# S5's reciprocal and stores placed anew, its scan laid out with group pairs innermost, biases and S5's copies on ScalarE, the last rows stored by halves

## What is computed

```
for layer in 0, 1:
    x = norm0(a * x + 0.5 * swiglu_1(x))
    x = norm1(a * x + mix(x))          # layer 0: MoBA attention || retention;  layer 1: S5 + GLU
    x = norm2(a * x + 0.5 * swiglu_2(x))
S5: lam_bar = exp(lam * dt);  b_bar = (lam_bar - 1) / lam * b
    s[t] = lam_bar * s[t-1] + b_bar u[t]   (64 groups x 64 complex states)
    y[t] = real(c s[t]) + d * u[t]
```

## Time and profile before

| | us |
|---|---|
| median of 3 runs | 2661.59 |
| the profiled execution: time | 2662.27 |
| its span (first to last instruction) | 2660.6 |
| PE busy | 2451.7 (92%) |
| DVE busy | 1674.6 (63%) |
| ACT busy | 1013.3 (38%) |
| POOL busy | 605.6 (23%) |
| mean granted TensorE clock | 0.965 |

### The profile page before, as it was taken

One profiled execution on the slowest core, in us unless ns is written; L12 is line 12 of the kernel. 1 busy time (PEld: TensorE's weight loads), 2 busy tenths in 40 slices (PEclk: granted clock), 3 DMA queues, 4 the chain that ended last, 5 costly groups with the idle time before them and its releaser, 6 DMA issues.

```text
span 2660.6 us, 45493 instructions
## 1 busy us (share of the span) xinstructions
PE 2451.7 (92%) x18333; PEld 2301.8 (87%) x18333; DVE 1674.6 (63%) x2676; ACT 1013.3 (38%) x1496; POOL 605.6 (23%) x658
## 2 busy tenths in 40 slices
PE   6998498999899889999999999999999979989995
PEld 6998497999788767779889999999999978989995
DVE  4786375657765544567676658567556685576554
ACT  2443134433354333344253433454333425343332
POOL 5487630000420012210121401023102220242003
PEclk9999799999999999999899999999999989999997
DMA  8657366543453678645446555555554646544452
GB/s 174 182 160 194 91 190 189 150 120 114 124 146 112 207 225 261 170 121 145 111 143 187 168 153 175 179 158 143 155 150 143 194 136 197 157 143 135 143 149 77
DMA packets 675394, 417.25 MB, mean 157 GB/s; under 512 B 31250, under 2 KB 639378, under 8 KB 675186
## 3 DMA queue, kind: packets, MB, share of 16 engines
q1 hardware_dynamic: 668658, 393.98, 51.6%
q0 software_dynamic: 6528, 20.37, 2.5%
HBM read 395.51 MB, written 18.78 MB: 156 GB/s over the span
## 4 chain that ended last, share of the span: by engine, by line
PE 70%; DVE 14%; POOL 5%; issue 4%; ACT 4%; DMA 3%; SPq 2%; POOLq 0%; ACTq 0%; DVEq 0%
PE ps L255 18%; PE ps L256 18%; PE ps L257 18%; DVE w_lo L250 3%; ACT w_hi L241 2%; PE ps L838 2%; PE ps L840 2%; PE ps L839 2%; POOL arena L1964 2%; PE ps L2192 1%; PE ps L1533 1%; POOL x L551 1%; PE ps L1548 1%; DVE arena L2292 1%; PE ps L1575 1%
## 5 line engine op out<-in xcount | busy, mean ns | idle before, releaser
L250 DVE TENSOR_TENSOR w_lo<-w_raw,w_hi 128x1024 fp32r<-128x1024 f32 (+1 forms) x648 | 821.3, 1273 | 658.7 <-ACT w_hi L241 655.1
L255 PE MATMUL ps<-x_hi,w_hi 128*128 128x256 f32 (+1 forms) x3200 | 973.3, 304 | 60.7 <-DVE w_lo L250 51.7
L256 PE MATMUL ps<-x_lo,w_hi 128*128 128x256 f32 (+1 forms) x3200 | 959.0, 300 | 0.0
L257 PE MATMUL ps<-x_hi,w_lo 128*128 128x256 f32 (+1 forms) x3200 | 958.2, 299 | 0.0
L241 ACT ACTIVATE w_hi<-w_raw 128x1024 fp32r<-128x1024 f32 (+1 forms) x648 | 668.3, 1034 | 561.3 <-PE ps L257 398.6
L255 PEld LDWEIGHTS ps<-x_hi,w_hi 128*128 128x128 f32 x3200 | 619.8, 194 | 78.2 <-DVE w_lo L250 64.8
L256 PEld LDWEIGHTS ps<-x_lo,w_hi 128*128 128x128 f32 x3200 | 619.9, 194 | 1.4 <-issue 0.2
L257 PEld LDWEIGHTS ps<-x_hi,w_lo 128*128 128x128 f32 x3200 | 619.1, 193 | 0.0
L255 PE MATMUL ps<-h_hi,w_hi 128*128 128x256 f32 (+1 forms) x1408 | 425.9, 303 | 15.7 <-DVE w_lo L250 11.1
L256 PE MATMUL ps<-h_lo,w_hi 128*128 128x256 f32 (+1 forms) x1408 | 416.0, 295 | 0.0
L257 PE MATMUL ps<-h_hi,w_lo 128*128 128x256 f32 (+1 forms) x1408 | 416.0, 295 | 0.0
(11 more groups left out here) (257 smaller groups left out, 2361.5 us busy)
## 6 DMA issues: line engine op xcount, KB each, us to landing
w_raw<-in_ffn_w_gate SPq DMA_DIRECT2D x176, 512.0 KB, 4.3
w_raw<-in_ffn_w_up SPq DMA_DIRECT2D x176, 512.0 KB, 3.9
w_raw<-in_ffn_w_down SPq DMA_DIRECT2D x128, 512.0 KB, 4.0
w_raw<-in_w_in_ab SPq DMA_DIRECT2D x56, 512.0 KB, 3.9
w_raw<-in_ffn_w_down SPq DMA_DIRECT2D x64, 384.0 KB, 3.4
arena<-in_cache_v POOLq DMA_DIRECT2D x64, 256.0 KB, 4.5
arena<-in_cache_k SPq DMA_DIRECT2D x64, 256.0 KB, 3.8
w_raw<-in_w_out_ab SPq DMA_DIRECT2D x16, 512.0 KB, 3.8
```

The source lines that it names most:

```text
L250: dve.tensor_tensor(T.w_lo[:, u % RING, 0:n], T.w_raw[:, u % RAW, 0:n], T.w_hi[:, u % RING, 0:n].bitcast(F32), ALU.subtract).then_inc(T.w_ ...
L255: pe.matmul(out, w_hi, m_hi, start=first, stop=False)
L256: pe.matmul(out, w_hi, m_lo, start=False, stop=False)
L257: return pe.matmul(out, w_lo, m_hi, start=False, stop=last)
```

## The change

1. `size2`'s reciprocal is made on DVE inside `S5Constants.vector` (four more small instructions there, three fewer on POOL), and the copies of the reversed powers go from step 10 to step 7 with a semaphore of their own, `fallen`. POOL makes `b_bar` first and waits for `fallen` afterwards. PE turns c at step 5 instead of 10.
2. `prepare.load` issues b in 16 DMAs of 32 KB, two a weave step, then c, in weave steps 0 to 8, where SP had only the weights. Decays are stored at lag -3 instead of 5, taps at lag 4.
3. `start` is laid out `[128, re/im, chunk, pair]`. `advance` has 6 instructions; the first product and the first sum take both parts at once. The carry is added run by run: DVE takes runs 0 and 1 (1 alone for A, whose first carry is zero), POOL runs 2 and 3.
4. ACT, instead of DVE, copies `u` from PSUM and makes both halves of `stack`.
5. ACT, instead of POOL, adds the bias in all twelve norms: at norm steps 5 and 6 behind DVE's scaling where no products follow, at steps 7 and 8 behind DVE's L511 otherwise (POOL did it at 8 and 9).
6. The very last norm (`alone`) sums its squares by 8 accumulating products with the ones matrix on PE, into another PSUM bank; POOL has no part in it.
7. The output goes by column halves: PE turns the first 4 feature tiles as soon as those have their bias, DVE and ACT copy by turns, SP stores 6 pieces for B.

```diff
@@ Norm
+            if i == 4 and self.alone:
+                for k in range(KT):
+                    pe.wait_ge(T.squared.h, self.squared + k + 1)
+                    pe.matmul(self.root_of, T.ones[:, :], T.sq[:, k % 4, 0:self.g.n], start=(k == 0), stop=(k == KT - 1))\
+                      .then_inc(T.sq_added.h, 1)
...
+            if i in (5, 6):
                 for k in range(4 * i - 20, 4 * i - 16):
                     act.wait_ge(T.normed.h, self.normed + k + 1)
...
+                        act.activation(self.x(k), self.x(k), ACT.Identity, bias=self.bias(k)).then_inc(T.affine_done.h, 1)
+            if i in (7, 8) and self.products:
+                for k in range(4 * i - 28, 4 * i - 24):
+                    act.wait_ge(T.x_ready.h, self.ready + k + 1)
+                    act.activation(self.x(k), self.x(k), ACT.Identity, bias=self.bias(k)).then_inc(T.affine_done.h, 1)
...
-                    pool.tensor_scalar(self.x(k), self.x(k), self.bias(k), None, ALU.add).then_inc(T.affine_done.h, 1)
@@ store
+    for i, (t, q, m) in enumerate(halves(g)):
         n = after + i
+        pe.wait_ge(T.affine_done.h, whole - 4 + 4 * q)
...
+        sp.wait_ge(T.y_moved[n % 2].h, n // 2 + 1)
+        dst = y_prompt[t * P:(t + 1) * P, :] if t < PT else y_sample
+        sp.dma_start(dst[:, q * 512:(q + 1) * 512], rows[0:m, t, q * 512:(q + 1) * 512]).then_inc(T.stored.h, 16)
@@ S5Prepare
-    TURN_C = 10
+    FALL, TURN_C = 7, 5
...
+        for n in range(KT):
+            a = slice(A4 * n, A4 * (n + 1))
+            for r, part in enumerate(("re", "im")):
+                q.dma_start(self.b_raw[:, r, a], self.I["s5_b_" + part][0].rearrange("(a s) p h -> (s p) a h", s=2)[:, a])\
+                 .then_inc(self.S.b_loaded.h, 16)
+            yield
...
-            q = self.at(i, 5)
+            q = self.at(i, -3)
             if q is not None:
                 sp.wait_ge(S.c_done.h, q + 1)
...
+            q = self.at(i, 4)
+            if q is not None:
                 sp.wait_ge(S.placed.h, q + 1)
...
-                pool.wait_ge(S.inverted.h, 1)
                 tt(S.coef[:, :, :], S.coef[:, :, :], S.size2[:, :].unsqueeze(1).to_broadcast([P, 2, GPAIRS]), ALU.mult)
...
+                pool.wait_ge(S.fallen.h, 1)
                 pool.wait_ge(S.c_placed.h, 1)
@@ S5Group
+        eng.tensor_tensor(both, src, f[0].unsqueeze(1).to_broadcast([P, 2, *shape]), ALU.mult)
+        eng.tensor_tensor(buf[0], src[:, 1], f[1], ALU.mult)
+        chain(eng, eng.tensor_tensor(buf[1], src[:, 0], f[1], ALU.mult))
+        chain(eng, eng.tensor_tensor(out, out, both, ALU.add))
+        eng.tensor_tensor(out[:, 0], out[:, 0], buf[0], ALU.subtract)
+        chain(eng, eng.tensor_tensor(out[:, 1], out[:, 1], buf[1], ALU.add))
...
+        for b in (0, 1):
+            if b or self.before is not None:
+                self.fix(dve, T.dve_chain, self.part, b)
             yield
...
+                for s in range(2):
+                    self.stack(act, copy, e + 1, s)
```

More of the change, by code:

```diff
@@ L450, with __init__ @@
     STEPS = 10
-    def __init__(self, T, g, row, scale, products):
+    def __init__(self, T, g, row, scale, products, alone=False):
+        self.alone = alone
         self.T, self.g, self.row, self.products = T, g, row, products
@@ L460, in __init__ @@
         self.sq_added, self.var, self.rooted, self.normed = (
-            c.take(k) for c, k in ((T.sq_added, KT - 1), (T.var_done, 1), (T.rstd_ready, 2), (T.normed, KT)))
+            c.take(k) for c, k in ((T.sq_added, KT if alone else KT - 1), (T.var_done, 1), (T.rstd_ready, 2), (T.normed, KT)))
         self.affine, self.rounded, self.ready = (
@@ L537, in gpsimd @@
         for i in range(self.STEPS):
-            if i in (1, 2):
+            if i in (1, 2) and not self.alone:
                 for k in range(max(4 * i - 4, 1), 4 * i):
@@ L2222, in stack @@
         for r in range(2):
-            last = copy(to[HALF[r], s], self.start[HALF[s], r, pairs, :])
+            last = copy(to[HALF[r], s], self.start[HALF[s], r, :, pairs].rearrange("p c a -> p a c"))
         last.then_inc(S.stacked[s].h, 1)
@@ L2272, in scalar @@
             if e is not None and e + 1 < KT:
-                self.stack(act, copy, e + 1, 0)
+                for s in range(2):
+                    self.stack(act, copy, e + 1, s)
             if self.before is not None:
@@ L2282, in scalar, with advance @@
             yield
-    def over(self, r, k, shape):
-        f = self.jump[:, r, k]
-        return f.unsqueeze(2).to_broadcast(shape) if len(shape) == 3 else f
-    def advance(self, eng, chain, buf, out, src, f):
-        for i, (r, w) in enumerate(((0, 0), (1, 0), (1, 1), (0, 1))):
-            last = eng.tensor_tensor(buf[i], src[r], f[w], ALU.mult)
-        chain(eng, last)
-        eng.tensor_tensor(out[0], out[0], buf[0], ALU.add)
-        chain(eng, eng.tensor_tensor(out[1], out[1], buf[1], ALU.add))
-        eng.tensor_tensor(out[0], out[0], buf[2], ALU.subtract)
-        chain(eng, eng.tensor_tensor(out[1], out[1], buf[3], ALU.add))
-    def bufs(self, place, shape):
+    def advance(self, eng, chain, place, out, src, f, shape):
         n = int(np.prod(shape))
@@ L2302, in bufs, with over, fix @@
         sizes = {f"d{i}": k for i, k in enumerate(shape)}
[L2303 to L2318 removed]
+        both = place[:, 0:2 * n].rearrange(f"p (r {names}) -> p r {names}", r=2, **sizes)
+        buf = [place[:, i * n:(i + 1) * n].rearrange(f"p ({names}) -> p {names}", **sizes) for i in (2, 3)]
+        eng.tensor_tensor(both, src, f[0].unsqueeze(1).to_broadcast([P, 2, *shape]), ALU.mult)
[4 more added lines that the diff above has]
+        chain(eng, eng.tensor_tensor(out[:, 1], out[:, 1], buf[1], ALU.add))
+    def over(self, k, shape):
+        f = [self.jump[:, r, k] for r in range(2)]
+        return [x.unsqueeze(1).to_broadcast([P, *shape]) for x in f] if len(shape) == 2 else f
+    def runs(self):
+        return self.start[:, :, 0:CHUNKS_P, :].rearrange("p r (b j) a -> p r b j a", j=RUN)
+    def fix(self, eng, chain, place, b):
+        runs, shape = self.runs(), [RUN - 1, GPAIRS]
+        self.advance(eng, chain, place, runs[:, :, b, 1:], runs[:, :, b, 0:1].to_broadcast([P, 2, *shape]),
+                     [self.jump[:, r, 0:RUN - 1] for r in range(2)], shape)
     def vector(self, dve):
@@ L2342, in vector @@
                                   ALU.subtract).then_inc(S.rested.h, 1)
-            e = self.out_at(i, 1)
-            if e is not None and e + 1 < KT:
-                self.stack(dve, dve.tensor_copy, e + 1, 1)
             yield
@@ L2379, in scan @@
         yield
-        for a0 in (0, self.FIX):
-            self.fix(dve, T.dve_chain, self.part, a0)
+        for b in (0, 1):
+            if b or self.before is not None:
+                self.fix(dve, T.dve_chain, self.part, b)
             yield
         if self.before is not None:
-            advance([self.ends[:, r].rearrange("p b a -> p a b") for r in range(2)],
-                    [self.start[:, r, :, CHUNKS_P:] for r in range(2)], 0, [P, GPAIRS, DEC_BATCH])
+            advance(self.ends, self.start[:, :, CHUNKS_P:, :], 0, DEC_BATCH, GPAIRS)
             dve.memset(self.part[:, 1023:1024], 0.0).then_inc(S.ends_done.h, 1)
@@ L2741, in _ @@
             load_tables(T, M, sp, I)
-            prepare.load(sp)
-            weave(ffn(ffn_sync, sp, f0a + f0b[:1]), after(idle(1 + KT), prepare.sync(sp)))
+            weave(ffn(ffn_sync, sp, f0a + f0b[:1]), after(prepare.load(sp), prepare.sync(sp)))
             run(project_sync(T, sp, PA))
@@ L2813, in _ @@
             weave(ffn(ffn_scalar, act, f3a[2:]), N4B.scalar(act))
-            weave(ffn(ffn_scalar, act, f3b), N5A.scalar(act))
-            run(N5B.scalar(act))
+            weave(ffn(ffn_scalar, act, f3b), after(N5A.scalar(act), store_scalar(T, act, A, y_rows, before[A])))
+            run(after(N5B.scalar(act), store_scalar(T, act, B, y_rows, before[B])))
         @block.vector
```

151 lines of the change are left out of this document (66 added, 85 removed).

## The result

The changed kernel takes **2605.24 us** (2602.03 to 2605.82) against 2663.13 for the kernel before beside it: a ratio of 0.978, 95% interval 0.976 to 0.979, or 57.9 us less. The forecast was 2583 us: faster, but with 79 us to gain. The profiled execution has a span of 2603.2 us (2660.6 before) and a mean granted clock of 0.975 (0.965 before). PE is busy 2446.0 us (2451.7 before), DVE 1638.9, ACT 1085.3 and POOL 470.4.

What follows compares the result with a forecast made beforehand. PE was taken as the bound, busy 2451.7 of 2660.6 us, with DVE the bound in B's scan. Terms 47 + 15.5 + 4.7 + 7 + 8 - 3 = 79 off 2662.3, less 0.7, gave 2583 us; range 2564 to 2612.

Steps and rivals of the forecast that it cites:

- The first stage: Beside the first feed-forward, up to the projection: loads, early powers, stores, clock and projection together save 47 us (35 to 54).
- Reversed powers early: -11.7: First feed-forward: POOL's earlier powers shrink PE's 21.6 us wait for residual sums to about 10, saving 11.7 us.
- the loads in pieces: Early first feed-forward: b's 16 pieces end a 6.9 us weight wait, 4.5 us plus 1.5 for half clock: -6.
- the step of the stores: First feed-forward: decays stored eight steps earlier, apart from the taps, no longer hold up weights on SP: -6.4 us.
- unhindered, octets 0 to 3: POOL's reversed powers in the first feed-forward: without hindrance, octets 0 to 3 done at 196 us, 21.4 us each.
- R1: Rival, 14%: POOL or SP keep the first stage slow, 24 us an octet; only 20 of 47 us come: 2610.
- B's scan: Shorter VectorE scan instructions and fixes, with ScalarE's share of stack and a little clock, save 15.5 us (9 to 20).
- The sign named for PE's idle time: In B's scan, PE's idle time was to fall from 20.0 to about 5 us.
- A's scan: Nearly covered by PE's longer steps; waits of 3.66 and 1.8 us show, so -4.7 us (2 to 5).
- what is late next: First feed-forward, once PE's wait for the sums shrinks to about 10 us: POOL's own work is late next.
- charged 3 us for everything: Biases on ACT delay its next rounding, for which DVE and PE wait: a cost of 3 us (0 to 10).
- R2: Rival, 12%: layout is nothing, strides cost nothing; B saves 5 us, A 2, so 13 less: 2596.

Runs made afterwards that it cites:

- run 2: Kernel before plus only b's loads in 16 pieces and the decays' and taps' stores placed anew: 2626.9 us, ratio 0.9861.
- run 3: Kernel before plus the early reciprocal and reversed powers, the loads in pieces and the stores placed anew, nothing else: 2620.9 us, ratio 0.9834.
- run 4: Kernel before plus only the new scan: layout of start, six instructions an advance, fix by runs; u and stack copies as before: 2652.0 us, ratio 0.9956.
- run 6: Changed kernel with the biases of all layer norms back on GpSimd: 2607.24 us, ratio 0.9789.
- run 1: Kernel before plus only the early reciprocal, with the copies of the reversed powers and the turn of c five steps earlier: 2664.79 us, ratio 1.0004.
- run 8: Changed kernel with start back in its old layout (chunks innermost), six instructions an advance and fix by runs kept: 2620.54 us, ratio 0.9833.
- run 5: Changed kernel with two of the four stack copies of an octet back on VectorE: 2602.62 us, ratio 0.9765.
- run 12: Changed kernel with some norms' biases back on GpSimd, B's fix signal earlier, stack copies on both engines except B's first octet (ScalarE): 2602.03 us, ratio 0.9769.

## Why the prediction was right and wrong

**The direction and the large terms held.** The total lies in the stated range (2564 to 2612 us) but at its slow end, outside the 2570 to 2596 that had 60%: 22 us of the 79 did not come. The first stage gave 39 of 47 us, the end 9.4 of 8, A's last norm 5.9 of 7, and the projection's part 8.1 of 7. The short instructions came out at 286 and 424 ns, for 290 and 420. A's last norm had some luck: the profile of the kernel before has PE waiting 4.31 us there, while runs 2, 3 and 4, which leave this norm alone, wait 2.0 to 2.7 and take 1.7 to 1.9 us less for the stretch. The biases are worth 4.0 by run 6 (68.6 against 64.6).

**The first stage: the wrong owner.** The step "Reversed powers early: -11.7" failed as an attribution. Run 2 has the shorter wait without the early powers, and run 1 has the early powers without any gain. The rows had said it: POOL waited 34.8 us for the powers but 64.0 for the decays, and the second wait lies later. An earlier start ahead of a later wait only lengthens that wait. The powers alone are worth 0, and 6 us on top of the stores.

**The first stage: 9 us short.** Two terms were too large; ScalarE's reads of a gate, the marks used in run 8, show where. At 65 us the changed kernel is 3.2 us ahead, where the loads in pieces were to give 6: PE's wait there fell from 6.92 to 2.16 us, but by 35 us the kernel had lost 1.6, as runs 1 and 2 do by themselves (1.5 and 1.3). From there to 258 us it gains 3.0 more, where the step of the stores had 6.4. PE's waits over 0.3 us between 70 us and its wait for the sum come to 13 us in both kernels: the 3.0 us at the taps and a wait of 2.2 went, and others took their place. POOL's forms are not free for VectorE, as I had them in "unhindered, octets 0 to 3". Between 112 and 154 us, where they now stand, the lead of 3.2 us turns into a lag of 1.3. Run 2, with late forms, keeps its lead of 4.3 there and loses it between 154 and 220 us. The early forms move that cost; only the run with the forms cut to a third takes it away, and its PE reaches the sum 13 us sooner. So PE came to the sum at 261.5 us and not near 255, and the sums were complete at 271.0 and not near 265. The wait of about 10 came out right (9.6) because both were late by the same 6 us, which is luck. In the second row PE shows a new wait of 1.77 us at 323 us, with a granted clock of 0.79 around it, in place of the 12.5. R1 did not come about: POOL's octets took 20 to 21 us and not 24.

**B's scan: 7.1 of 15.5.** The run of the scan alone gives 11.3. So 4 us of the term were never there, and 2.7 of them are the two fixes: I put them at 6.5 us, near their undisturbed length, and beside POOL's they take 5.7 and 3.5. Another 4 were taken by the parts moved to ScalarE. The reads of the gate show where: in the norm ahead of the scan the changed kernel loses 3.2 us, and run 6, with the biases on GpSimd, loses none. From the eighth read to the sixteenth the scan then gains 10.2 us (11.3 in run 4), and 11.6 with two of the stack copies back on VectorE (run 5), where I had charged 0.7 for them. In run 12 it gains 14.7. The sign named for PE's idle time, from 20.0 to about 5, did not come: it is 16.3, and the clock brought more than the waits did.

**A's scan: -5.8 where 4.7 was due.** By the same reads 3.6 us of it are lost in the norm at the stretch's start, by the stand of 3.78 us at 1452 us and the dry PE behind it: the other kernels with these biases on ScalarE lose 2.8 to 3.6 there, and run 6 loses nothing. The scan's own part is nothing. From the fifteenth read of this stretch to the sixteenth, where the scan ends, it is 50.6 us in run 4 and 51.4 in the changed kernel, against 49.3 to 50.9 in the kernel before and run 3. POOL's pair of fixes, 14 us long, took over as the last to end. That is the question "what is late next", which I had put for the first stage and not for A's scan. The prediction saw that ScalarE takes on 2 to 2.5 us a step in the norms without products and charged 3 us for everything; it is in these norms that PE ran dry, and the two scan stages alone measured 6.2 (run 6), so this term was too small.

**R2 was wrong.** The Trainium skill, "VectorE: DVE Perf Modes", section on the TRN2 errata, gives by its formula 291 and 424 ns (its figures, worked out as an estimate). The contiguous instructions agree (286 and 424), the strided ones do not (393 and 655, run 8). The formula has the number of elements in it and nothing else; "whatever the layout" in the prediction was my reading of that, and the measurement decides against it. In this kernel the layout is nearly the whole of the scan's gain (run 8).

**The end: right, within the spread.** Squares on PE took 7.5 us within the 6.5 to 11.5 named. From the sum's product to the end of the squares' products it is 9.4 us in place of 10.7 before: 1.3 for the 1 forecast. The last bias ended 0.6 us behind VectorE, where 0.5 was forecast.

## What to carry to other kernels

When an engine waits twice in one stretch, cost each release by the later wait: ending the earlier one alone was worth nothing here. When work moves to an idle engine, ask what is queued behind it there and what it does to its neighbour's instructions; the same move can pay in one place and cost in another, so decide it for each place. When a signal is moved ahead of some work, check that no reader of it sits in the same queue behind that work.

## What the runs showed of the hardware

- **Strided float32 operands cost VectorE time.** With chunks innermost, so that neighbouring elements of an operand lie a whole row of chunks apart, 128 elements take 393 ns and 256 take 655; with group pairs innermost, 286 and 424. That is 107 and 231 ns more, 0.8 to 0.9 ns an element.
- **VectorE's instructions with two operands in SBUF grow beside GpSimd's, those that read PSUM do not.** A rest of 1024 elements takes 1.23 us alone, 1.98 beside the forms and 1.40 beside a third of them, while `prod<-gate,ps` stays at 421 ns. A cast with one operand in SBUF grows too, from 0.29 to 0.47 us (at 2150.41 us in B's scan). The Trainium skill, "SBUF — State Buffer", section "Who interferes with whom", says that a VectorE instruction with two SBUF inputs and a GpSimd instruction that reads SBUF exclude each other; the trace agrees for these two (1.98 us against 421 ns).
- **The same end of the kernel took 20.4 to 24.9 us** in kernels that do not change it, with stretches of half clock at different places in it: the median product of the squares takes 432 ns in run 5 (21.7 us to the end) and 741 ns in the changed kernel (23.7). A difference of 1 or 2 us there needs more than one profile.
